# A hybrid decoder layer on one core: input rows, front order and squares of the mixing stage rearranged

## What is computed

```python
h = rmsnorm(x, g_mix)
q, fg, inp, og, cb, cc, ch, ga, gb = split(h @ w_in)          # nine blocks of 1024 columns
logf = logaddexp(log(lb), log1p(-lb) + log_sigmoid(fg))        # lb is 0 with one layer
kf = (1 - lb) * sigmoid(-fg)
o, s_new = hgrn2_scan(silu(q), kf, inp, logf, state)           # 8 heads, decayed linear attention
o = rmsnorm(o, g_hg_out) per head * silu(og)
y_a = o @ w_br_a
y_b = (cb * conv3(cc * ch)) @ w_br_b
x = x + (sigmoid(ga) * y_a + sigmoid(gb) * y_b) @ w_out
x = x + hier_moe(rmsnorm(x, g_ffn))                            # 32 experts, 2 per token
x = x + sigmoid(rmsnorm(x, g_ple) @ w_ple_gate) * (p @ w_ple_proj)
y = rmsnorm(x, g_final)
```

## Time and profile before

| | us |
|---|---|
| median of 3 runs | 1377.08 |
| lowest, highest | 1368.84, 1377.29 |
| profiled execution, its own time | 1377.8 |
| span of its instructions | 1376.1 |
| mixing block, to about | 875 |
| experts, about | 990 to 1283 |

### The profile page before, as it was taken

The page is one execution under the profiler, slowest core; times in us unless marked ns, Lnnn a source line. Parts: engine busy times, 40 slices in busy tenths (PEclk is TensorE's granted clock), DMA queues, the critical chain, the costliest instruction groups (busy, mean ns, idle before and its releaser), DMA issues. The chain is left out here.

```text
span 1376.1 us, 14804 instructions
## 1 busy us (share of the span) xinstructions
PE 1236.5 (90%) x5963; PEld 865.9 (63%) x5963; DVE 481.8 (35%) x1042; ACT 233.6 (17%) x410; POOL 102.1 (7%) x163
## 2 busy tenths in 40 slices
PE   4989999999998999998999999988499877888596
PEld 3855888887776488886777788544355444444242
DVE  3141376135204255513321210155323222222375
ACT  2222121011003231001103100011112122212122
POOL 0000000000000000000000000001223222221000
PEclk9989999998998999999989999999589999999898
DMA  6111101231211111212333533301479999995300
GB/s 229 62 61 62 51 26 47 77 96 50 92 65 60 61 61 62 77 48 79 96 121 82 215 129 148 128 31 43 156 295 385 382 396 393 395 394 225 130 31 34
DMA packets 78492, 191.81 MB, mean 139 GB/s; under 512 B 10918, under 2 KB 29174, under 8 KB 70232
## 3 DMA queue, kind: packets, MB, share of 16 engines
q1 hardware_dynamic: 72984, 181.91, 36.2%
q0 software_dynamic: 5440, 8.94, 2.0%
HBM read 180.71 MB, written 17.98 MB: 144 GB/s over the span
## 5 line engine op out<-in xcount | busy, mean ns | idle before, releaser
L946 PE MATMUL ps<-arena,weights 128*128 128x272 f32 x2560 | 623.6, 406 | 16.8 <-DVE arena L731 13.2
L946 PEld LDWEIGHTS ps<-arena,weights 128*128 128x128 f32 x2560 | 501.7, 197 | 135.6 <-DVE arena L731 14.1
L1392 PE MATMUL ps<-arena 128*64 128x256 f32 x1024 | 131.0, 414 | 32.9 <-DMA arena<-in_w_up 32.8
L1392 PEld LDWEIGHTS ps<-arena 128*64 128x64 f32 x1024 | 76.9, 149 | 76.2 <-DMA arena<-in_w_up 35.5
L662 DVE TENSOR_SCALAR arena<-arena 128x544 f32<-128x544 f32 x32 | 14.2, 444 | 182.9 <-ACT arena L640 98.9
L1112 PE MATMUL ps<-weights,arena 128*128 128x512 f32 (+1 forms) x160 | 68.3, 630 | 2.1 <-PEq L424 2.1
L1653 PE MATMUL ps<-weights,arena 128*128 128x512 f32 (+1 forms) x160 | 64.6, 605 | 1.3 <-DVE arena L1716 1.3
L1484 DVE TENSOR_SCALAR arena<-arena 64x256 f32<-64x256 f32 x32 | 9.2, 289 | 158.8 <-ACT arena L1445 151.0
L1405 PE MATMUL ps<-arena 128*64 128x512 f32 x256 | 61.9, 604 | 0.6 <-DVE arena L1508 0.6
L981 PE MATMUL ps<-arena 128*128 128x64 f32 x448 | 55.1, 277 | 0.6 <-DVE arena L772 0.6
L981 PEld LDWEIGHTS ps<-arena 128*128 128x128 f32 x448 | 53.8, 194 | 2.4 <-DVE arena L772 1.1
(11 more groups left out here) (219 smaller groups left out, 1046.3 us busy)
## 6 DMA issues: line engine op xcount, KB each, us to landing
weights<-in_w_in SPq DMA_DIRECT2D x18, 2048.0 KB, 8.1
arena<-in_w_gate SPq DMA_DIRECT2D x32, 1024.0 KB
arena<-in_w_up SPq DMA_DIRECT2D x32, 1024.0 KB
arena<-in_w_down SPq DMA_DIRECT2D x32, 1024.0 KB
arena<-in_x_prompt SPq DMA_DIRECT2D x8, 512.0 KB, 8.3
arena<-in_state_hgrn SPq DMA_DIRECT2D x8, 512.0 KB, 9.8
out_hgrn_sample<-arena SPq DMA_DIRECT2D x8, 512.0 KB, 3.6
weights<-in_w_br_b SPq DMA_DIRECT2D x2, 2048.0 KB, 7.8
```

Of the source, the lines that this page charges most:

```text
L946: ins = mm(ps[:, b + s, 0:HF], W[:, c % 2, k, col:col + P], src[:, k, s * HF:s * HF + HF], start=(k == 0), stop=(k == KT - 1))
L1392: ins = mm(ps[u * UP:u * UP + CAP, 2 + s, 0:DE], xgT[s][:, k, :], w[e % 4][:, k, :], start=(k == 0), stop=(k == KT - 1))
```

## The change

- **Start.** The identity and the small rows are issued by ScalarE; SyncE begins with the input rows. ScalarE does one tiny Square first (on `half_r`), then the five squares. DVE copies the small rows out first, then makes 1/rms of tiles 0 and 1, scales these, makes 1/rms of tiles 2 to 4, and ScalarE scales those.
- **Front.** In both halves value tiles 0 and 1 follow `gates`, then the new events `gexp` (the Exp that was the end of `gates` on ScalarE) and `kprep` (the keys' part of `qprep`), then value tiles 2 to 4, the query tiles, and `qprep`, which keeps one product.
- **Squares.** A new event `sq` holds DVE's square; `stat` keeps the rest. `sq` stands a tile or more ahead of its `stat`, with three buffers for heads 0 to 3. The weave of the second half is regrouped for it.

```diff
     def front(g):
-        return [*tiles("fg", g), ("gates", g), *tiles("q", g), ("qprep", g),
-                *[("v", (g, t)) for t in range(NT)]]
+        v = [("v", (g, t)) for t in range(NT)]
+        return [*tiles("fg", g), ("gates", g), *v[0:2], ("gexp", g), ("kprep", g), *v[2:], *tiles("q", g), ("qprep", g)]
...
-    ev += weave(attention(1), tiles("gb", 0) + tiles("yb", 0) + tiles("gb", 1) + yb[0:2] + [("stat", 0), ("stat", 1), yb[2],
-                              ("norm", 1), ("stat", 2), ("stat", 3), yb[3], ("norm", 3)] + tiles("og", 0), 1.0)
+    ev += weave(attention(1), tiles("gb", 0) + tiles("yb", 0) + tiles("gb", 1) +
+                [yb[0], ("sq", 0), yb[1], ("sq", 1), yb[2], ("stat", 0), ("stat", 1), ("sq", 2), ("norm", 1), ("sq", 3),
+                 yb[3], ("stat", 2), ("stat", 3), ("norm", 3)] + tiles("og", 0), 1.0)
     for j in (4, 6):
-        ev += [("ga", j - 4), ("stat", j), ("stat", j + 1), ("ga", j - 3), ("norm", j + 1)]
+        ev += [("sq", j), ("sq", j + 1), ("ga", j - 4), ("stat", j), ("stat", j + 1), ("ga", j - 3), ("norm", j + 1)]
...
+        def squares_of(x):
+            return SG[:, (0, 1, 2, 0)[x], :] if x < 4 else squares1[:, x % 2, :]
...
@@ SyncE @@
-                sp.dma_start(ident[:, :], a["c_ident"]).then_inc(id_loaded, 16)
                 for t in range(NT):
...
-                for i, (name, r0) in enumerate((("g_mix", 0), ("g_hg_out", 8), ("g_ple", 16))):
-                    sp.dma_start(rows[r0:r0 + 8, :], a[name].rearrange("o (r p) -> (o r) p", p=P)).then_inc(rows_loaded, 16)
-                sp.dma_start(rows[24:48, :], a["w_conv"].rearrange("o j (r p) -> (o j r) p", p=P)).then_inc(rows_loaded, 16)
-                sp.dma_start(cs[0:16, :], a["state_conv"].rearrange("o b j c -> (o b j) c")).then_inc(rows_loaded, 16)
...
@@ ScalarE @@
+                act.dma_start(ident[:, :], a["c_ident"]).then_inc(id_loaded, 16)
...
                 from_dve()
+                link(nc.scalar.activation(half_r[:, :], ss[:, :], ACT.Square))
+                for x in range(NT):
+                    n = TOK[x]
+                    act.wait_ge(x_loaded[x], 16)
+                    nc.scalar.activation(R["X"][0:n, 0:D], xt[0:n, x, :], ACT.Square, accum_out=ss[0:n, x:x + 1]).then_inc(a2d, 1)
+                    act.wait_ge(a2d, x + 1)
+                from_dve()
+                for x in range(2, NT):
+                    n = TOK[x]
+                    nc.scalar.activation(xt[0:n, x, :], xt[0:n, x, :], ACT.Copy, scale=rs[0:n, x:x + 1]).then_inc(a2p, 1)
...
                         nc.scalar.activation(Kl, qc, ACT.Ln, bias=eps[:, 1:2]).then_inc(a2d, 1)
+                    elif kind == "gexp":
                         from_dve()
                         nc.scalar.activation(X, X, ACT.Exp).then_inc(a2d, 1)
-                    elif kind == "qprep":
+                    elif kind == "kprep":
                         from_dve()
                         nc.scalar.activation(qc, cum, ACT.Exp).then_inc(a2d, 1)
...
@@ DVE @@
+                            for t in range(2):
+                                from_act()
+                                dve.wait_ge(x_loaded[t], 16)
+                            rstd(v, link, ss[:, 0:2], rs[:, 0:2])
+                            scaled(0)
+                            scaled(1)
+                            for t in range(2, NT):
+                                from_act()
+                            rstd(v, link, ss[:, 2:NT], rs[:, 2:NT])
+                            v.engine_nop().then_inc(d2a, 1)
...
                     elif kind == "qprep":
+                        link(v.tensor_tensor(qc, qc, Q, ALU.mult))
+                    elif kind == "kprep":
+                        from_act()
                         dve.wait_ge(dve_step, step.n)
                         v.engine_nop().then_inc(d2a, 1)
...
-                        from_act()
-                        link(v.tensor_tensor(qc, qc, Q, ALU.mult))
-                        from_act(), from_act(), from_act()
+                        for _ in range(4):
+                            from_act()
                         v.tensor_tensor(Kl, Kl, X, ALU.mult).then_inc(kt_ready, 1)
...
-                    elif kind == "stat":
+                    elif kind == "sq":
...
-                        if x % 4 >= 2:
-                            after_tile(dve, "stat", x - 2)
-                        sq = SG if x < 4 else squares1
-                        v.tensor_tensor(sq[:, x % 2, :], oT[:, x, :], oT[:, x, :], ALU.mult).then_inc(d2p, 1)
+                        if x in (3, 6, 7):
+                            after_tile(dve, "stat", {3: 0, 6: 4, 7: 5}[x])
+                        v.tensor_tensor(squares_of(x), oT[:, x, :], oT[:, x, :], ALU.mult).then_inc(d2p, 1)
+                    elif kind == "stat":
...
@@ TensorE @@
-                        from_dve()
+                        if x < 2:
+                            from_dve()
+                        else:
+                            pe.wait_ge(a2p, x - 1)
```

More of the change, by code:

```diff
@@ L541, in from_dve @@
                     act.wait_ge(d2a, d2a_n.next())
-                from_dve()
-                for kind, x in ev:
-                    if kind == "xT":
-                        n = TOK[x]
-                        act.wait_ge(x_loaded[x], 16)
-                        nc.scalar.activation(R["X"][0:n, 0:D], xt[0:n, x, :], ACT.Square, accum_out=ss[0:n, x:x + 1]).then_inc(a2d, 1)
-                        act.wait_ge(a2d, x + 1)
-                    elif kind == "fg":
+                act.dma_start(ident[:, :], a["c_ident"]).then_inc(id_loaded, 16)
+                for i, (name, r0) in enumerate((("g_mix", 0), ("g_hg_out", 8), ("g_ple", 16))):
+                    act.dma_start(rows[r0:r0 + 8, :], a[name].rearrange("o (r p) -> (o r) p", p=P)).then_inc(rows_loaded, 16)
+                act.dma_start(rows[24:48, :], a["w_conv"].rearrange("o j (r p) -> (o j r) p", p=P)).then_inc(rows_loaded, 16)
+                act.dma_start(cs[0:16, :], a["state_conv"].rearrange("o b j c -> (o b j) c")).then_inc(rows_loaded, 16)
+                from_dve()
+                link(nc.scalar.activation(half_r[:, :], ss[:, :], ACT.Square))
[8 more added lines that the diff above has]
+                    nc.scalar.activation(xt[0:n, x, :], xt[0:n, x, :], ACT.Copy, scale=rs[0:n, x:x + 1]).then_inc(a2p, 1)
+                for kind, x in ev:
+                    if kind == "fg":
                         b, freed = waits_tile(act, kind, x)
@@ L681, in _ @@
                         if x == 0:
-                            for t in range(NT):
-                                from_act()
-                                dve.wait_ge(x_loaded[t], 16)
-                            rstd(v, link, ss[:, :], rs[:, :])
-                            scaled(0)
-                        if x + 1 < NT:
-                            scaled(x + 1)
-                        if x == 0:
                             dve.wait_ge(rows_ready, 1)
@@ L1034, in _ @@
                         for s in range(2):
-                            ins = mm(ps[:, b + s, 0:HF], ones[:, :], (SG if x < 4 else squares1)[:, x % 2, s * HF:s * HF + HF], start=True, stop=True)
+                            ins = mm(ps[:, b + s, 0:HF], ones[:, :], squares_of(x)[:, s * HF:s * HF + HF], start=True, stop=True)
                         ins.then_inc(tile_ready[n % 2], 1)
```

## The result

The changed kernel takes 1336.24 us (median of 4 runs, 1325.61 to 1340.05); the kernel before, on the same chip, 1372.96 (4 runs, 1368.42 to 1377.29). The ratio is 0.973, 95% interval 0.969 to 0.977. The profiled execution of the changed kernel took 1340.05 us with a span of 1338.3; its sum in the prediction was 1342.4.

The account below looks back on a forecast made before the run. TensorE, busy 1236.5 of 1376.1 us, was taken as the bound. Savings of 5.6 (start) + 19.2 (fronts) + 5.1 + 5.5 (squares) = 35.4 us gave 1342.4, or 1341.7 for the median; range from 1331, its top covering 1352.

Parts of the forecast that it names:

- Fronts: Both halves: the wait for the query release and the slow pair behind it go, 9.6 us each, together 19.2.
- rival B: Lower clock not the waits' doing (slow pair at 238.97 without wait): fronts save 13.2, not 19.2; 1348.7; chance 0.10.
- D: Rival: TensorE falls to 1.2 GHz in each of the fronts' 26 tiles, 2.5 us each: 1406.7; chance 0.02.
- E: Rival: gate chain, 5.9 us later than worked out, holds value tiles 3 us in each half: 1347.7; chance 0.07.
- The first level: After the query tiles: ready after 9.4 us, wanted after 10.1; no wait, 0.7 us to spare.
- Start: First projection matmul comes at 20.9 instead of 26.52 us, a saving of 5.6.
- I take 6.5, nearer the low end: Start: the small rows' landing time, chosen between 5.0 and 10.2 us.
- rival A: Start: small rows land with the input, saving 1.9 in place of 5.6 us: 1345.4; chance 0.14.
- the price "of 1.06": Start: eight TensorE transposes of an input tile take 1.06 us, used in the chain from rsqrt to projection.
- Squares: Stat tiles: squares a tile earlier remove TensorE's waits for them, saving 5.1 us in the weave and 5.5 at ga.
- its two clock terms: At the ga pairs: slow stat matmuls and slow tiles behind them, 3.0 us of the saving, 1.0 from the tiles.
- C: Rival: expert stage ends when it ends now, so the shorter mix is given back: 1377, no change; chance 0.04.

Follow-up runs that it names:

- e1: Kernel before with only the front reorder (values between gates and queries, both halves): 1353.51 us, ratio 0.989.
- e3: Kernel before with only the squares put a step ahead: 1363.16 us, ratio 0.995.
- e5: The changed kernel unedited, measured again beside the kernel before: 1337.3 us, ratio 0.974.
- e2: Kernel before with only the changed start: 1367.51 us, ratio 0.999.
- e4: Changed kernel with all value tiles behind the whole gate chain: 1363.57 us, ratio 0.995.
- e11: Changed kernel with identity and small rows issued by SyncE ahead of the input rows, none by ScalarE: 1339.92 us (one run).
- e6: Changed kernel with DVE's copies of the small rows moved behind both rsqrts: 1338.26 us, ratio 0.975.
- e7: Changed kernel with one tiny Ln on ScalarE ahead of each stat pair: 1333.93 us, ratio 0.973.
- e9: Changed kernel with each head's state increment moved one projection tile later, ahead of the next head's stA: 1357.21 us, ratio 0.991.

## Why the prediction was right, and where it was not

**Fronts: right.** Forecast 9.6 and 9.6, measured 9.7 and 9.7, and in e1 9.7 and 9.7 too. Both the wait and the slow pair behind it went; no pair in either front of the changed kernel takes 18 us. So rival B, that the lower clock was not the waits' doing, falls for these pairs. The 3 us of lower clock in the price are not firm, though: e3 lost 1.6 behind the same wait and its old front took 98.2. And B's observation stays true elsewhere: the tiles behind heads still fall with no wait. D, falls all through the fronts, did not come. E falls by the margin: forecast 2.9 us spare at the fifth value tile, found 3.0 (77.82 against 80.78). The first level had 0.7 spare by the forecast; DVE's last pass ends at 123.25 and TensorE starts on it at 124.11, 0.9 later.

**Start: wrong, forecast 5.6, measured 2.7 (1.8 in e5, 3.2 in e2; 1.5 to 3.2 over all traces of this start order).** The step that failed is "I take 6.5, nearer the low end, since they are 0.1 MB on a queue of their own". The rows landed at 9.15 to 9.82 in every kernel that issues them from ScalarE. The Trainium skill's rule (Trainium Kernel Development and Optimization, Key Constraints) is that other queues save only the issue time. My estimate by it was 9.4 and a saving of 2.8; the trace agrees, and rival A was the truer case for this term. The value was taken near the low end for a reason (a queue of its own) that no row bore. The rest of the chain was right in the changed kernel's own profile: forecast 12.6 us from the first rsqrt to the projection, measured 12.36 (23.81 - 11.45). It holds only in some traces, since the price "of 1.06" for eight transposes does: the last 24 take 2.8 us in the changed kernel, e2 and e4, and 4.03 to 4.66 in e5 to e11. So the same chain takes 13.8 us in e5 (24.74 - 10.94), and in e6 the second rsqrt comes 2.9 us earlier but the first forget tile only 1.1.

**Squares: right mechanism, undersized, forecast 10.6, measured 12.6.** The waits went as worked out: 0.17 left in the weave (forecast 0.2), 1.16 at ga twice (forecast 1.2), 3.22 us from ga tile to ga tile (687.65 - 684.43; forecast 3.2). The table load takes 1.28 and in e7 stands 0.02 us behind the tanh and 0.01 ahead of the next ACTIVATE. The Trainium skill (ScalarE: Activation LUTs, What ACT_TABLE_LOAD costs) has a drain of 1.38 us beside the load; the trace of e7 does not show it.

The view by stretches, of the kernel before and the changed one over the squares' stretch (bounds, length, busy time of each engine, granted clock, DMA):

```profile
481.40:782.10 300.70, 289.94 (x1406) 238.17 (x1405) 108.79 (x158) 53.72 (x72) 6.92 (x7) 0.95 0.26 87
```

```profile
454.30:742.40 288.10, 284.98 (x1405) 234.98 (x1404) 112.42 (x161) 53.47 (x71) 6.94 (x7) 0.96 0.27 90
```

TensorE stood 10.8 us before and stands 3.1 now: 7.6 less, which is what the forecast comes to without its two clock terms (the slow stat matmuls of 2.84 and 3.23, and the slow tiles behind them). The other 5.0 us are busy time, and of those the forecast had 3.0. The 2.0 more lie in the scatter of that stretch, which is 297.4 in e2 and 303.9 in e1 with the same old squares. The total of e3, 6.2 us with an interval to 12.0, speaks for less than 12.6.

**The rest.** C falls: 382.7 before, 382.5 after; the expert stage starts earlier and runs as before. The sum of 35.4 against 37.8 measured is closer than its terms deserve, and that is luck: the start gave 2.9 less, and the middle stretch, for which I forecast nothing, 4.9 more. The median came 5.5 us under the forecast of 1341.7; 4.1 of that is the kernel before, whose median is 1372.96 over four runs and was 1377.08 over three.

Where the 4.9 come from: the view by stretches, of the kernel before, the changed one and e1, over the middle stretch (bounds, length, busy time of each engine, granted clock, DMA).

```profile
126.20:380.90 254.70, 252.56 (x1247) 208.28 (x1246) 105.61 (x173) 35.06 (x77) 6.94 (x7) 0.94 0.21 68
```

```profile
113.80:363.50 249.70, 247.53 (x1245) 205.04 (x1243) 109.21 (x176) 34.91 (x76) 6.95 (x7) 0.96 0.21 69
```

```profile
116.40:362.70 246.30, 244.18 (x1245) 203.60 (x1243) 109.08 (x176) 34.84 (x76) 6.94 (x7) 0.97 0.22 70
```

TensorE stands 2.1 to 2.2 us in all three. What differs is the granted clock. With two levels, the lower half the higher, a mean of 0.94 loses 0.06 of the length: 15.3, 10.0 and 7.4 us here. The differences, 5.3 and 2.6 us, match the 5.0 and 3.4 by which the lengths differ, as closely as a clock of two digits can (1.3 us each). The tiles say where: over the undisturbed times, the 32-row matmuls and the tile (or pair) behind each of the four heads take 11.7, 10.0 and 6.6 us more in all. So the changed kernel and e1 differ by falls behind heads, and the kernel before has in addition the fall of 2.5 us at 238.97. The profiled execution of before had many: at 1377.8 it lies 8 us over the 1369.35 of 25 runs on the chip of e1 to e3, so the pair of traces shows a little more (37.8) than the medians do (36.7 and, with e5, 35.8).

## What to carry to other kernels

When TensorE waits for a buffer, look at what stands ahead of the release on the releasing engine; here two 0.6 us copies in each half, put between the steps of a long chain, made 26 us between e4 and the changed kernel. Price a load by what shares the transfers with it, not by the queue that issues it. Work moved into a gap leaves the place it came from: check what waited there. And look for parts of under 1% in their own stretch of the trace, with the standing time apart from the slow tiles, in more than one trace: the start shows how a gain at one event can be gone at the next.

## What the runs showed of the hardware

- The time lost to the lower clock (1.2 in place of 2.4 GHz) behind a wait was 3.1 and 2.9 us after 6.5 and 6.7 us in the kernel before, 1.6 after 6.5 in e3, 1.9 and 1.8 after 10.8 and 10.9 in e4, and nothing measurable after 1.16.
- TensorE also falls with no wait: behind thin matmuls (4 columns, 32 rows) four matmuls take 3.50 in place of 1.98, and the tile behind 9.41 in place of 7.5. In e9, with a tile in between, it still takes 9.25 behind the 4-column ones alone. How many heads are hit changes between executions and is part of the scatter of 9 to 18 us between runs of one kernel.
- The granted clock as printed does not tell all at the start. The first four forget tiles take 29.57 us in the changed kernel and 32.53 in e11, and both read 1.00 there; in e4 they take 31.26 and read 0.95. Whether the 3 us in e11 are lower clock that the record misses was not shown. So look at the duration of equal tiles, not at the clock alone.
- Six small loads behind 2.1 MB landed at 11.59, beside them from another queue at 9.15 to 9.82, ahead of them at 4.83.
